# A trunk kernel: modulation rows computed four parts at a time, the first rows of h made in halves, and a pooling band matmul of 144 columns

## The chip, the cores and the metric

The kernel runs on one core of a Trainium2 chip. The metric is the device time of one execution in microseconds. The kernel before takes 1817.61 us (median of 3 runs, 1816.09 to 1818.15).

## The reference, cut to what matters

1024 tokens of 1024 features, two layers, all in float32. Each sub-layer normalizes, scales and shifts by rows made from one conditioning vector `c` (the modulation), and adds its gated result to x.

```python
c_act = jax.nn.silu(c)
for l in range(2):
    mod = c_act @ w_ada[l] + b_ada[l]          # (1, 6 * 1024), six parts
    sh_m, sc_m, g_m, sh_f, sc_f, g_f = jnp.split(mod, 6, axis=-1)
    h = rmsnorm(x, norm_mix_g[l]) * (1 + sc_m) + sh_m
    if l == 0:   # one projection to 2560 columns, gating in chunks of 128, a conv of width 3, w_out
        y = concat(chunk_sgu(u, v), short_gated_conv(b, c, x_in)) @ w_out_even[0]
    else:        # per group of 256 channels: mean over the last 2/4/8/16 tokens minus h, then a 256x256 map
        y = pool_mixer(h, w_pool[0], pool_scale[0])
    x = x + g_m * y
    h = rmsnorm(x, norm_ffn_g[l]) * (1 + sc_f) + sh_f
    x = x + g_f * hier_moe(h, ...)             # 32 experts, two per token
return rmsnorm(x, final_norm_g)
```

## The kernel before, in words

The program is written engine by engine, with semaphores between them; on each engine and each DMA queue the order is the order of the code. Large products are taken in a high part and a rest (names with `_hi`/`_lo`, "high" and "low" in the trace), three matmuls for one. There are six stages.

1. Start (to 42 us): x is loaded, squared and scaled on ScalarE, transposed on TensorE into `hT` ("h_columns"); VectorE sums the first two modulation parts.
2. Making h (to 67.5 us). For each of 8 blocks k of 128 features, [128 x 1024 tokens]: ScalarE writes the high part `h_hi`; VectorE writes the modulated `hT` in place (L1054) and, for even k, the rest `h_lo` (L1058); GpSimd writes `h_lo` for odd k (L645), as well as the rest of each weight piece (`piece_low`, L639). TensorE's first unit of the projection follows block by block.
3. Projection (to about 261 us). 16 pieces of weights w, two token halves each, so 32 units u of 24 matmuls of 512 columns (L1524 to L1526). ScalarE evicts units 0 to 23 (L837), loads the next piece and makes its high part. Beside it runs the modulation: ten parts, each of eight 512 KB loads on SP's queue (L486, `cond_w`, four buffers) and eight VectorE multiply-adds over [128 x 1024] (L1079). A part is then summed over the partitions by TensorE (`sum_part`, L1504, matmuls against ones), behind the unit that `PART_BEHIND` names (4, 6, 8, 10, 13, 15, 17, 19, 22, 24), and written out by ScalarE (`part_row`), some of them after VectorE has applied a gain (L1067). The load of the v weights on SP waits for the last sum.
4. v, the gating, the output projection, the residual and the rows for the experts, a tile of 128 tokens at a time.
5. The experts of layer 0 (to about 1055 us), then the pooling stage (1063 to 1152 us), then the experts of layer 1 and the last norm.
6. Of the pooling stage, iteration k works on several tiles. VectorE: `combine` of tile k (L1419, L1420), scaling of h for tile k-1 (L1433) and its shift (L1436, then `h_ready`), the entry rows for tile k-3 (L1150, L1152), the residual of tile k-2 (L1442). TensorE: band matmuls of tile k-1, for each of 8 blocks one of 128 columns (L1738) and one of 16 columns with the tile before (L1741), transposes and router logits of older tiles, then the group map of tile k-1 (L1754), which waits for `pool_kept` and for the residual of the tile before. ScalarE: squares, one eviction of the pooled columns (L996), eviction of transposes.

Of the kernel before, what the change touches and what calls it, by code (L numbers as in the profile page):

```python
# [45 lines left out]
def hybrid_trunk(nc, x, c, w_ada, b_ada, norm_mix_g, norm_ffn_g, w_in_even, sgu_norm_g, w_spatial,  # L46
# [6 lines left out]
    P = 128  # L53
# [48 lines left out]
    with ctx:  # L102
# [9 lines left out]
        C0 = T0 + 16 * KB + 256  # L112
# [6 lines left out]
        def small(name, shape, dt=F32):  # L119
            n = 4  # L120
            for s in shape[1:]:
# [19 lines left out]
        acc = [at(f"cond_acc{q}", [P, D], X0 + 4 * q * KB) for q in range(2)]  # L141
        bias = [at(f"cond_bias{q}", [P, D], X0 + (8 + 4 * q) * KB) for q in range(2)]
        CONDS = 4
        cond = [at(f"cond_w{q}", [P, D], X0 + (16 + 4 * q) * KB) for q in range(CONDS)]
        gain_in = at("gain_row_in", [1, D], T0 + 8 * KB)
        row_kept = at("mod_row", [1, D], T0 + 4 * KB)

        PARTS = [(0, m) for m in range(2, NMOD)] + [(1, m) for m in range(NMOD)]
        N0 = NMOD - 2
        GAIN_OF = {(0, SC_F): (norm_ffn_g[0:1, :], 1.0), (1, SC_M): (norm_mix_g[1:2, :], 1.0),  # L150
                   (1, G_M): (pool_scale[0:1, :], 0.0), (1, SC_F): (norm_ffn_g[1:2, :], 1.0)}
        GAINED = [n for n, q in enumerate(PARTS) if q in GAIN_OF]
        STORED = [n for n, q in enumerate(PARTS) if q not in ((0, G_M), (0, G_F))]

        PART_BEHIND = {4 + 9 * n // 4: n for n in range(len(PARTS))}


# [50 lines left out]
        band = at("band", [P, PG, P], T0 + 12 * KB)  # L208
        band0 = at("band_first", [P, PG, P], T0 + 14 * KB)
        band_prev = at("band_previous", [P, PG, REACH], T0 + 16 * KB)  # L210
# [73 lines left out]
        vec_rows = at("vector_rows", [P, P], T0)  # L284
        vec = small("vector_columns", [P, 64])
        c_e = small("c_exp", [P, KD])
        c_act = small("c_act", [P, KD])
# [34 lines left out]
        vc = vec[:, KD:2 * KD]  # L322
        NVEC = 2 * KD + 3 * KA

        def conv_col(k, m):
            return vec[:, 2 * KD + k * KA + m:2 * KD + k * KA + m + 1]
# [7 lines left out]
        PM = BANK[6]  # L334
        PL = BANK[7]
# [8 lines left out]
        bias_loaded = [sem(f"bias_loaded{q}") for q in range(2)]  # L344
# [7 lines left out]
        pool_loaded, rows1_loaded = sem("pool_loaded"), sem("rows1_loaded")  # L352
        rows0_loaded, ffn1_loaded = sem("rows0_loaded"), sem("ffn1_loaded")
# [19 lines left out]
        h_act, h_dve, h_pool = sem("h_act"), sem("h_dve"), sem("h_pool")  # L373
# [38 lines left out]
        h_ready, pool_T, pool_kept = sem("h_ready"), sem("pool_T"), sem("pool_kept")  # L412
# [7 lines left out]

        def h_made(k):

            return k + (k + 1) // 2 + 1
# [33 lines left out]
        def _(sp):  # L457
# [3 lines left out]
            sp.dma_start(vec_rows[2 * KD:NVEC, :],  # L461
# [16 lines left out]
            def part_loads(n):  # L478
                l, m = PARTS[n]
                if n >= 2:  # L480
                    sp.wait_ge(cond_used, KD * (n - 1))
# [16 lines left out]
            for n in range(len(PARTS)):  # L498
                part_loads(n)
            sp.wait_ge(part_summed, len(PARTS))  # L500
# [9 lines left out]
            for part, q0, n in zip(out_parts, (0, 4, 6, 7), (4, 2, 1, 1)):  # L510
                sp.dma_start(part[:, :, :], ow[:, q0:q0 + n, :]).then_inc(out_w_loaded, 16)
            sp.wait_ge(v_done, NT)
            sp.wait_ge(row_stored, 16 * len(STORED))
# [85 lines left out]
        def _(pool):  # L599
# [30 lines left out]
            g.sem_inc(consts, 1)  # L630
            pool.wait_ge(x_T, NT)
            for q in range(2):
                note(g.memset(bias[q][:, :], 0.0))
# [8 lines left out]
            piece_low(0)  # L642
            for k in range(1, KD, 2):
                pool.wait_ge(h_dve, h_made(k))
                g.tensor_tensor(h_lo[:, k, :], hT[:, k, :], h_hi[:, k, :].bitcast(F32), ALU.subtract).then_inc(h_pool, 1)  # L645
            for w in range(1, PIECES):
                piece_low(w)
# [24 lines left out]
            def bands():  # L672
# [17 lines left out]
                note(g.tensor_copy(band0[:, :, :], band[:, :, :]))  # L690
# [39 lines left out]
            for l in range(LAYERS):  # L730
                if l:
                    pool.wait_ge(h_ready, NT)
                    pool.wait_ge(x_mixed1, YB + 1)
                    clear_gathered()
# [35 lines left out]
        def _(act):  # L770
# [6 lines left out]

            act.wait_ge(vec_ready, 1)
            a.activation(c_e[:, :], vc, ACT.Exp, scale=-1.0).then_inc(c_exp_ready, 1)
# [21 lines left out]

            act.wait_ge(mod_ready0, 1)
# [6 lines left out]
            def load_gain(i):  # L809
                src = GAIN_OF[PARTS[GAINED[i]]][0]  # L810
                act.dma_start(gain_in[0:1, :], src).then_inc(gain_loaded, 16)
# [971 lines left out]
```

## Time and profile before

| | us |
|---|---|
| median of 3 runs | 1817.61 |
| profiled execution, its own time | 1813.75 |
| its span, first to last instruction | 1811.9 |
| TensorE busy | 1639.3 |
| VectorE busy | 1510.0 |
| ScalarE busy | 1030.9 |
| GpSimd busy | 437.1 |

The profile shows one execution. Busy shares are averages over stages with different limits, so what a change is worth is read from the stages that it touches. "Idle before <- X" tells how long an engine stood still and what released it. The clock column is the granted TensorE clock, 1.00 for 2.4 GHz and 0.50 for 1.2 GHz.

### The profile page before, as it was taken

To read this page: it belongs to the slowest core of one execution; us is meant where nothing else is said; L and a number is where in the kernel's file an instruction comes from. 1 tells how busy PE (TensorE), PEld (TensorE's weight loads), DVE (VectorE), ACT (ScalarE), POOL (GpSimd) and SP (SyncE) were. 2 spreads that over 40 slices of the span, in tenths; PEclk is the share of its full clock that TensorE was granted. 3 is DMA by queue.
4 is the path that set the end of the run, shared out by engine and by line. 5 is a ranking of instruction groups with operands and counts; after the bars stand their busy time and mean duration, and the time that the engine had idled before them with its cause. 6 is when DMAs were issued, how large, how long until landed. Compare 5 with 4: busy or idle time off the path is not lost. (4 is left out here: it accounts for less than half of the span.)

```text
span 1811.9 us, 20023 instructions
## 1 busy us (share of the span) xinstructions
PE 1639.3 (90%) x7847; PEld 1371.4 (76%) x7847; DVE 1510.0 (83%) x1095; ACT 1030.9 (57%) x840; POOL 437.1 (24%) x227
## 2 busy tenths in 40 slices
PE   3799999996899999999999949699999999999980
PEld 3577787785788888888888749678888888888870
DVE  5988785644699999999999758679999999999966
ACT  7221112322467777777777524357777777777742
POOL 1412130220424232322223100003432322233210
PEclk8799999997799999999999969789999999999995
DMA  9699712314699999999999954169999999999947
GB/s 340 203 314 314 266 69 81 119 46 197 218 343 376 381 385 390 385 383 387 381 388 388 387 210 173 49 234 365 381 388 387 387 383 384 384 384 387 386 183 285
DMA packets 125270, 547.62 MB, mean 302 GB/s; under 512 B 24003, under 2 KB 42975, under 8 KB 76021
## 3 DMA queue, kind: packets, MB, share of 16 engines
q1 hardware_dynamic: 91934, 497.98, 72.6%
q0 software_dynamic: 18432, 33.60, 4.9%
q10 hardware_dynamic: 14808, 14.73, 2.4%
q8 instruction: 64, 1.05, 0.2%
q14 instruction: 32, 0.26, 0.0%
HBM read 533.61 MB, written 46.17 MB: 320 GB/s over the span
## 5 line engine op out<-in xcount | busy, mean ns | idle before, releaser
L1310 DVE TENSOR_TENSOR unit_low<-unit,unit_high 128x2048 fp32r<-128x2048 f32 x384 | 856.0, 2283 | 15.3 <-ACT unit_high L924 15.0
L924 ACT ACTIVATE unit_high<-unit 128x2048 fp32r<-128x2048 f32 x384 | 735.4, 1915 | 42.6 <-DMA unit<-in_moe_w_up_dram 17.6
L1621 PE MATMUL ps<-unit_high,block_columns_high 128*128 128x512 f32 x1024 | 407.2, 398 | 10.4 <-DVE block_columns_low L1315 10.4
L714 POOL DMA_INDIRECT expert_rows<-y_out,assignment x64 | 214.8, 3357 | 804.3 <-DVE y_out L1340 791.9
L1623 PE MATMUL ps<-unit_high,block_columns_low 128*128 128x512 f32 x1024 | 401.2, 392 | 0.0
L1622 PE MATMUL ps<-unit_low,block_columns_high 128*128 128x512 f32 x1024 | 400.8, 391 | 0.0
L1621 PEld LDWEIGHTS ps<-unit_high,block_columns_high 128*128 128x128 f32 x1024 | 194.3, 190 | 50.2 <-DVE block_columns_low L1315 11.8
L1623 PEld LDWEIGHTS ps<-unit_high,block_columns_low 128*128 128x128 f32 x1024 | 193.5, 189 | 41.5
L1622 PEld LDWEIGHTS ps<-unit_low,block_columns_high 128*128 128x128 f32 x1024 | 193.8, 189 | 38.3
L1633 PE MATMUL ps<-unit_high,act_columns_high 128*128 128x512 f32 x512 | 206.7, 404 | 9.8 <-DVE unit_low L1310 9.8
L1635 PE MATMUL ps<-unit_high,act_columns_low 128*128 128x512 f32 x512 | 201.6, 394 | 0.0
L1634 PE MATMUL ps<-unit_low,act_columns_high 128*128 128x512 f32 x512 | 201.4, 393 | 0.0
L943 ACT ACTIVATE act_columns_high<-ps 128x512 fp32r<-128x512 f32 x64 | 38.4, 599 | 187.6 <-PE ps L1641 187.6
L708 POOL DMA_INDIRECT gathered<-normed_rows,token x64 | 110.7, 1730 | 140.5 <-issue 72.8
L1079 DVE SCALAR_TENSOR_TENSOR cond_acc<-cond_w,c_act,cond_acc 128x1024 f32<-128x1024 f32 x70 | 114.2, 1631 | 21.4 <-DMA cond_w<-in_w_ada_dram 14.2
L1315 DVE TENSOR_TENSOR block_columns_low<-ps,block_columns_high 128x1024 fp32r<-128x1024 f32 x64 | 78.2, 1222 | 53.5 <-ACT block_columns_high L873 53.3
L1524 PE MATMUL ps<-h_columns_high,in_w_high 128*128 128x512 f32 x256 | 107.8, 421 | 13.8 <-POOL h_columns_low L645 7.8
L1633 PEld LDWEIGHTS ps<-unit_high,act_columns_high 128*128 128x128 f32 x512 | 97.5, 190 | 28.6 <-issue 10.1
L1635 PEld LDWEIGHTS ps<-unit_high,act_columns_low 128*128 128x128 f32 x512 | 97.1, 190 | 20.9
L1634 PEld LDWEIGHTS ps<-unit_low,act_columns_high 128*128 128x128 f32 x512 | 97.4, 190 | 18.7
L1526 PE MATMUL ps<-h_columns_high,in_w_low 128*128 128x512 f32 x256 | 102.2, 399 | 0.0
L1525 PE MATMUL ps<-h_columns_low,in_w_high 128*128 128x512 f32 x256 | 102.1, 399 | 0.0
(225 smaller groups left out, 1962.6 us busy)
## 6 DMA issues: line engine op xcount, KB each, us to landing
unit<-in_moe_w_gate_dram SPq DMA_DIRECT2D x128, 1024.0 KB, 7.7
unit<-in_moe_w_up_dram SPq DMA_DIRECT2D x128, 1024.0 KB, 7.3
unit<-in_moe_w_down_dram SPq DMA_DIRECT2D x128, 1024.0 KB, 8.5
cond_w<-in_w_ada_dram SPq DMA_DIRECT2D x80, 512.0 KB, 5.2
y_in<-expert_rows SPq DMA_DIRECT2D x16, 1024.0 KB, 7.3
x_rows<-in_x_dram SPq DMA_DIRECT2D x8, 1024.0 KB, 9.9
cond_w<-in_w_ada_dram SPq DMA_DIRECT2D x8, 1024.0 KB, 11.1
in_w<-in_w_in_even_dram ACTq DMA_DIRECT2D x12, 512.0 KB, 7.9
```

The costliest lines, as they stand in the source:

```text
L708: g.indirect_dma_start(out=dst[:, :], out_offset=None, in_=xn_dram[l], in_offset=bass.IndirectOffsetOnAxis(ap=index, axis=0), bounds_check ...
L714: g.indirect_dma_start(out=y_dram[l], out_offset=bass.IndirectOffsetOnAxis(ap=index, axis=0), in_=src[:, :], in_offset=None, bounds_check= ...
L924: a.activation(high[k][:, :], raw[i % SLOTS][:, :], ACT.Copy).then_inc(unit_high, 1)
L1079: ch.link(v.scalar_tensor_tensor(out=acc[n % 2][:, :], in0=cond[k % CONDS][:, :], scalar=c_act[:, k:k + 1], in1=acc[n % 2][:, :] if k else ...
L1310: v.tensor_tensor(low[i % SLOTS][:, :], raw[i % SLOTS][:, :], high[k][:, :].bitcast(F32), ALU.subtract)\
L1524: mm(BANK[u % 4], w_hi, h_hi[:, k, tokens], start=k == 0, stop=False)
L1621: mm(dst, xT_hi[:, q, :], high[k][:, cols], start=q == 0, stop=False)
L1622: mm(dst, xT_hi[:, q, :], low[i % SLOTS][:, cols], start=False, stop=False)
L1623: last = mm(dst, xT_lo[:, q, :], high[k][:, cols], start=False, stop=q == KD - 1)
L1633: mm(BANK[2 + half], aT_hi[:, q, :], high[k][:, cols], start=q == 0, stop=False)
L1634: mm(BANK[2 + half], aT_hi[:, q, :], low[i % SLOTS][:, cols], start=False, stop=False)
L1635: last = mm(BANK[2 + half], aT_lo[:, q, :], high[k][:, cols], start=False, stop=q == KF - 1)
```

## The change

- Modulation: the ten parts become three groups (`QUADS`) of four, four and two parts. In a buffer of [128 x 1024] each part has 32 (or 64) partitions of its own, filled by one DMA per part. The vector c is laid out to match (six more small loads on ScalarE's queue at the start). A group is summed by matmuls against a [128 x 4] or [128 x 2] matrix behind units 13, 21 and 24, its rows are finished by one VectorE operation and stored by one DMA from SP. There are five buffers in place of four. The gain rows of layer 0 are read back from DRAM.
- Making h: by token halves. ScalarE also modulates `hT` for odd k, VectorE makes all of `h_lo` and the rest of pieces 0 and 1. The first units run in the order (piece 0, half 0), (1, 0), (0, 1), (1, 1).
- Pooling: one matmul of 144 columns per block; its last 16 columns are the next tile's share, which ScalarE keeps in `carry` and VectorE adds to the next tile's pooled columns (`pool_whole`). The shift of h is on GpSimd.
- In layer 0 the router logits of tile k-2 stand ahead of the transposes of tile k-1.

The core of the diff:

```diff
-                sp.dma_start(bias[n % 2][0:1, :], b_ada[l:l + 1, m * D:(m + 1) * D]).then_inc(bias_loaded[n % 2], 16)
-                for k in range(KD):
-                    if KD * n + k >= CONDS:
-                        sp.wait_ge(cond_used, KD * n + k - CONDS + 1)
-                    sp.dma_start(cond[k % CONDS][:, :],
-                                 w_ada[l].rearrange("(k p) n -> k p n", p=P)[k, :, m * D:(m + 1) * D])\
-                      .then_inc(cond_loaded[k % CONDS], 16)
+                for g in range(D // rows):
+                    if i >= CONDS:
+                        sp.wait_ge(cond_used, i - CONDS + 1)
+                    for j in range(parts):
+                        sp.dma_start(cond[i % CONDS][j * rows:(j + 1) * rows, :],
+                                     w_ada[l, g * rows:(g + 1) * rows, (m0 + j) * D:(m0 + j + 1) * D])\
+                          .then_inc(cond_loaded[i % CONDS], 16)
+                    i += 1
...
+            for n, (l, m0, parts) in enumerate(QUADS):
+                sp.wait_ge(row_out, n + 1)
+                sp.dma_start(mod_dram[l][m0:m0 + parts, :], mod_rows[n][0:parts, :]).then_inc(row_stored, 16)
+            sp.wait_ge(part_summed, len(QUADS))
...
+                    for t in range(NT):
+                        pool.wait_ge(h_scaled, t + 1)
+                        g.tensor_tensor(h_r[t % 2][:, :], h_r[t % 2][:, :], b1b[:, :], ALU.add).then_inc(h_ready, 1)
...
-                    a.activation(pooledT[:, :, :], PA[0].rearrange("p (k q) -> p k q", q=P), ACT.Copy)\
-                     .then_inc(pool_kept, 1)
+                    for q0, n in ((0, 6), (6, 2)):
+                        dst = pooledT[:, q0:q0 + n, :]
+                        last = a.activation(dst.rearrange("p (b q) c -> p b q c", q=3) if n == 6 else dst,
+                                            span_of(q0, n, slice(0, P)), ACT.Copy)
+                    last.then_inc(pool_kept, 1)
+                    for q0, n in ((0, 6), (6, 2)):
+                        dst = carry[(k - 1) % 2][:, q0:q0 + n, :]
+                        last = a.activation(dst.rearrange("p (b q) c -> p b q c", q=3) if n == 6 else dst,
+                                            span_of(q0, n, slice(P, SPAN)), ACT.Copy)
+                    last.then_inc(carry_kept, 1)
...
+            for half in range(2):
+                tokens = slice(half * CH, (half + 1) * CH)
+                for b in range(KD // 2):
+                    k = 2 * b
+                    dve.wait_ge(h_act, 12 * half + 3 * b + 1)
+                    v.tensor_scalar(hT[:, k, tokens], hT[:, k, tokens], a_m[:, k:k + 1], mod_c[:, SH_M, k:k + 1],
+                                    ALU.mult, ALU.add).then_inc(h_dve, 1)
+                    if b:
+                        dve.wait_ge(h_act, 12 * half + 3 * b)
+                        h_rest(k - 1, half)
+                    dve.wait_ge(h_dve, 4 * half + b + 1)
+                    h_rest(k, half)
...
-                    ch.link(v.scalar_tensor_tensor(out=h_r[t % 2][:, :], in0=xr[:, t, :],
-                                                   scalar=rstd[:, N_MIX1, t:t + 1], in1=a1b[:, :],
-                                                   op0=ALU.mult, op1=ALU.mult))
-                    v.tensor_tensor(h_r[t % 2][:, :], h_r[t % 2][:, :], b1b[:, :], ALU.add).then_inc(h_ready, 1)
+                    v.scalar_tensor_tensor(out=h_r[t % 2][:, :], in0=xr[:, t, :],
+                                           scalar=rstd[:, N_MIX1, t:t + 1], in1=a1b[:, :],
+                                           op0=ALU.mult, op1=ALU.mult).then_inc(h_scaled, 1)
+                if 2 <= k < NT + 1:
+                    t = k - 1
+                    dve.wait_ge(pool_kept, t + 1)
+                    dve.wait_ge(carry_kept, t)
+                    v.tensor_tensor(pooledT[:, :, 0:REACH], pooledT[:, :, 0:REACH], carry[1 - t % 2][:, :, :], ALU.add)\
+                     .then_inc(pool_whole, 1)
                 if 0 <= k - 3:
                     entry_rows(1, k - 3)
...
                     for q in range(KD):
-                        g = q // 2
-                        part = PA[0][:, q * P:(q + 1) * P]
-                        last = mm(part, h_r[t % 2][:, q * P:(q + 1) * P], (band if t else band0)[:, g, :],
-                                  start=True, stop=t == 0)
-                        if t:
-                            last = mm(part[:, 0:REACH], h_r[1 - t % 2][:, q * P:(q + 1) * P], band_prev[:, g, :],
-                                      start=False, stop=True)
+                        last = mm(span_cols(q), h_r[t % 2][:, q * P:(q + 1) * P],
+                                  (band_all if t else band0_all)[:, q // 2, :], start=True, stop=True)
```

## Rows read from the trace of the kernel before

**Rows 1.** Timeline of the pooling stage, VectorE (start us, duration us, instruction).
```profile
1102.14 1.28 DVE L1433 SCALAR_TENSOR_TENSOR h_rows<-x_rows,rstd,scale_row 128x1024 f32<-128x1024 f32 x1
1103.46 1.23 DVE L1436 TENSOR_TENSOR h_rows<-h_rows,shift_row 128x1024 f32<-128x1024 f32 x1
1105.28 0.17 DVE L1147 RECIPROCAL rstd<-root_mean_square 128x1 f32<-128x1 f32 x1 [0.60 <-ACT root_mean_square L776]
...
1111.66 1.28 DVE L1433 SCALAR_TENSOR_TENSOR h_rows<-x_rows,rstd,scale_row 128x1024 f32<-128x1024 f32 x1
...
1145.48 1.22 DVE L1442 TENSOR_TENSOR x_rows<-x_rows,ps 128x1024 f32<-128x1024 f32 x1
```

**Rows 2.** Timeline of the pooling stage, TensorE.
```profile
1071.49 3.75 PE L1738 MATMUL ps<-band_first,h_rows 128*128 128x128 f32 x16 [19.64 <-DVE h_rows L1436]
...
1106.53 0.38 PE L1738 MATMUL ps<-band,h_rows 128*128 128x128 f32 x2
1106.75 0.29 PE L1741 MATMUL ps<-band_previous,h_rows 128*128 128x16 f32 x2
...
1112.68 3.70 PE L1754 MATMUL ps<-pool_w,pooled_columns 128*128 128x256 f32 x16
1116.22 0.38 PE L1738 MATMUL ps<-band,h_rows 128*128 128x128 f32 x2
```

**Rows 3.** Timeline of the projection, VectorE.
```profile
62.42 1.27 DVE L1079 SCALAR_TENSOR_TENSOR cond_acc<-cond_w,c_act,cond_bias 128x1024 f32<-128x1024 f32 x1
...
76.96 2.81 DVE L1079 SCALAR_TENSOR_TENSOR cond_acc<-cond_w,c_act,cond_acc 128x1024 f32<-128x1024 f32 x1 [0.52 <-DMA cond_w<-in_w_ada_dram]
...
218.39 1.21 DVE L1067 SCALAR_TENSOR_TENSOR mod_row<-ps,gain_row_in 1x1024 f32<-1x1024 f32 x1 [0.36 <-DVE cond_acc L1079]
```

**Rows 4.** Busy times by window: us, PE, PEld, DVE, ACT, POOL, clock, DMA, GB/s.
```profile
47.70:67.50 19.80, 11.95 (x25) 7.42 (x26) 19.40 (x13) 5.63 (x6) 13.47 (x5) 0.50 0.39 134
...
100.00:130.00 30.00, 30.00 (x123) 22.77 (x122) 24.54 (x17) 6.07 (x9) 5.90 (x3) 1.00 0.92 318
```

**Rows 5.** Timeline from making h on, all engines.
```profile
43.23 9.15 ACT L805 ACTIVATE h_columns_high<-h_columns,mod_columns,a_mix 128x1024 fp32r<-128x1024 f32 x8
...
46.34 1.23 DVE L1058 TENSOR_TENSOR h_columns_low<-h_columns,h_columns_high 128x1024 fp32r<-128x1024 f32 x1
...
49.05 3.26 DVE L1058 TENSOR_TENSOR h_columns_low<-h_columns,h_columns_high 128x1024 fp32r<-128x1024 f32 x1
...
61.70 0.80 DVE L1054 TENSOR_SCALAR h_columns<-h_columns,a_mix,mod_columns 128x1024 f32<-128x1024 f32 x1
...
65.95 0.80 PE L1524 MATMUL ps<-h_columns_high,in_w_high 128*128 128x512 f32 x1 [2.27 <-POOL h_columns_low L645]
```

**Rows 6.** Timeline of the projection, ScalarE: evictions of units 2 and 3.
```profile
79.27 0.60 ACT L837 ACTIVATE conv_in<-ps 128x512 f32<-128x512 f32 x1 [3.54 <-PE ps L1526]
84.71 0.60 ACT L837 ACTIVATE conv_in<-ps 128x512 f32<-128x512 f32 x1 [4.84 <-PE ps L1526]
```

**Rows 7.** Timeline of TensorE: the sums behind units 19 and 24.
```profile
187.49 2.85 PE L1504 MATMUL ps<-cond_acc,ones 128*128 128x512 f32 x4 [2.61 <-DVEq L1084]
...
219.95 1.88 PE L1504 MATMUL ps<-cond_acc,ones 128*128 128x512 f32 x4
```

**Rows 8.** DMA issue of line 486 (ns), a window of 1 us, page's GB/s.
```profile
L486 SPq DMA_DIRECT2D cond_w<-in_w_ada_dram x80: 327/328/595, 47.8 to 212.3; - x80
...
229.00:230.00 1.00, 1.00 (x6) 0.85 (x5) 1.00 (x1) 0.00 (x0) 1.00 (x1) 1.00 1.01 345
...
GB/s 340 203 314 314 266 69 81 119 46 197 218 343 376 381 385 390 385 383 387 381 388 388 387 210 173 49 234 365 381 388 387 387 383 384 384 384 387 386 183 285
```

**Rows 9.** Timelines of GpSimd and ScalarE: an unhindered GpSimd subtraction, the pooled eviction.
```profile
176.08 2.39 POOL L639 TENSOR_TENSOR in_w_low<-in_w,in_w_high 128x1024 fp32r<-128x1024 f32 x1 [12.45 <-ACT in_w_high L799]
...
1083.59 1.02 ACT L996 ACTIVATE pooled_columns<-ps 128x1024 f32<-128x1024 f32 x1 [5.93 <-PE ps L1741]
```

**Rows 10.** A window of 2 us in the pooling stage, columns as in group 4.
```profile
1094.00:1096.00 2.00, 2.00 (x6) 1.65 (x5) 1.97 (x3) 1.62 (x4) 0.00 (x0) 0.50 0.96 330
```

More of the change, by code:

```diff
@@ L630, in _ @@
             g.sem_inc(consts, 1)
+            for i, tile in enumerate((pick4, pick2)):
+                note(g.memset(tile[:, :], 0.0))
+            for tile in mod_rows:
+                note(g.memset(tile[:, :], 1.0))
+            settle()
+            for parts in (4, 2):
+                for j in range(parts):
+                    rows = P // parts
+                    note(g.memset(pick[parts][j * rows:(j + 1) * rows, j:j + 1], 1.0))
+                settle()
             pool.wait_ge(x_T, NT)
-            for q in range(2):
-                note(g.memset(bias[q][:, :], 0.0))
+            for tile in acc:
+                note(g.memset(tile[:, :], 0.0))
             settle()
@@ L640, in piece_low @@
                                 piece_hi[w % HRING][:, :, :].bitcast(F32), ALU.subtract).then_inc(w_low, 1)
[L642 to L646, printed above, removed]
+            for w in range(2, PIECES):
                 piece_low(w)
@@ new lines, in _ @@
+            for half in range(2):
+                tokens = slice(half * CH, (half + 1) * CH)
+                for b in range(KD // 2):
+                    k = 2 * b
[7 more added lines that the diff above has]
+                    h_rest(k, half)
+                    if half == 0 and b == 1:
+                        piece_low(1)
+                dve.wait_ge(h_act, 12 * half + 12)
+                h_rest(KD - 1, half)
@@ new lines, in quad_sum @@
+            def quad_sum(n, i):
+                l, m0, parts = QUADS[n]
+                dve.wait_ge(bias_loaded, 16 * sum(q[2] for q in QUADS[:n + 1]))
+                for g in range(D * parts // P):
+                    dve.wait_ge(cond_loaded[i % CONDS], 16 * sum(PARTS_OF[i % CONDS:i + 1:CONDS]))
+                    ch.link(v.scalar_tensor_tensor(out=acc[n][:, :], in0=cond[i % CONDS][:, :],
+                                                   scalar=c_of[parts][:, g:g + 1], in1=acc[n][:, :],
@@ L1093, in conv @@
+            i = 0
+            for n in range(len(QUADS)):
+                i = quad_sum(n, i)
+                if n:
+                    quad_rows(n - 1)
+            quad_rows(len(QUADS) - 1)
             def conv(m):
@@ new lines, in project @@
+                if u >= 4:
+                    done = u - 3
+                    pe.wait_ge(*((proj_kept, done) if done <= 6 * KA else (z_kept, done - 6 * KA)))
+                tokens = slice(half * CH, (half + 1) * CH)
+                for k in range(KD):
+                    if u in (0, 2):
+                        pe.wait_ge(h_low, half * KD + k + 1)
+                    w_hi, w_lo = piece_hi[w % HRING][:, k, :], piece_lo[w % RING][:, k, :]
+                    mm(BANK[u % 4], w_hi, h_hi[:, k, tokens], start=k == 0, stop=False)
+                    mm(BANK[u % 4], w_hi, h_lo[:, k, tokens], start=False, stop=False)
+                    last = mm(BANK[u % 4], w_lo, h_hi[:, k, tokens], start=False, stop=k == KD - 1)
@@ L1531, in _ @@
+                last.then_inc(proj_done, 1)
+                if u in QUAD_BEHIND:
+                    sum_quad(QUAD_BEHIND[u])
             pe.wait_ge(x_T_kept, NT)
             pe.wait_ge(mod_ready0, 1)
-            for w in range(PIECES):
-                project(w)
+            for u in range(2 * PIECES):
+                project(u)
             pe.wait_ge(ws_loaded, 16)
-            pe.wait_ge(row_out, len(PARTS))
+            pe.wait_ge(row_out, len(QUADS))
             for h in range(HEADS):
@@ L1582, in _ @@
             pe.wait_ge(conv_done, 1)
-            for k in range(NT + 2):
+            for k in range(NT + 1):
                 if k < NT:
```

264 lines of the change are left out of this document (120 added, 144 removed).

## The prediction, made before the change was run

> **What bounds the kernel now.** I read the busy times by window first, then the timeline of each stage that the change touches, engine by engine, and asked who is late last in each. Three stages matter.
>
> In the making of h TensorE runs at 1.2 GHz (clock 0.50) and is busy 11.95 of 19.80 us, VectorE 19.40 [rows 4]. TensorE's last gap there ends with GpSimd's rest at 65.95 [rows 5]. VectorE's own rests take 1.23 us where GpSimd is quiet and share 3.26 us with it otherwise (the second is at 49.05) [rows 5]: the two engines hinder each other, so GpSimd's help costs VectorE almost as much as it takes over.
>
> In the projection two streams run side by side and end together. TensorE needs 5.44 us for a unit (84.71 - 79.27) [rows 6]. The modulation stream on VectorE starts at 62.42 and ends at 218.03, where the last gained row waits 0.36 us before 218.39 [rows 3]: 155.6 us for 80 multiply-adds, 1.945 us each. One alone takes 1.27 us, one beside GpSimd 2.81 us, and VectorE also waits for loads [rows 3]; in a window of this stage the DMA engines are 0.92 busy at 318 GB/s and VectorE is busy 24.54 of 30 us [rows 4]. TensorE already waited 2.61 us for that stream before the sum at 187.49 [rows 7], and starts the last sum at 219.95, which ends at 221.8 [rows 7].
>
> In the pooling stage TensorE is the bound, barely. From one tile's band matmuls to the next it takes 9.69 us (1116.22 - 1106.53) [rows 2]. VectorE's period, from scaling to scaling, is 9.52 us with 0.60 us of waiting in it [rows 1], so 8.9 us of work. The reader is to see here that VectorE runs ahead of the band matmuls: it hands h over and goes on to older tiles.
>
> **The change, part by part.**
>
> *Start.* Six small loads on ScalarE's queue and a larger transpose. What is late next there are the x loads and the first weights; I take 0, with 0 to 1.5 us as bounds (six issues of 0.33 us at most are 2 us, the price of an issue in [rows 8]).
>
> *Making h in halves.* A half of a block is 512 columns: for VectorE about 0.7 us for a rest (1.23 for 1024) and 0.45 for a modulation (0.80 for 1024) [rows 5]. A half of h is 8 x 0.7 + 4 x 0.45 = 7.4 us, with 1.2 us for the rest of piece 1 and 0.6 us of handoffs 9.2 us for the first half and 8 us for the second. ScalarE has 12 passes of 0.60 us [rows 6] and one of about 1.0 us per first half, 8.2 us: just ahead. ScalarE began at 43.23 in the old kernel [rows 5], behind the high part of piece 0, which is now made earlier; so VectorE starts near 42.5, the first half is there at 51.7, the second at 59.9. GpSimd is quiet, so nothing is hindered. TensorE ends unit 0 near 53, unit 1 near 60.3 (its first matmuls at the low clock), unit 3 near 71.3. It was at 84.7 [rows 6]: 13 us ahead.
>
> *Modulation.* Still 80 multiply-adds over [128 x 1024] and the same bytes. Gone are seven of ten sums on TensorE: 7 x 1.88 = 13 us [rows 7], ScalarE's row passes, and all but one row operation inside VectorE's stream. Without waits TensorE would end unit 24 at 71.3 + 21 x 5.44 + 2 x 1.88 = 189.3. But the stream decides. Its first multiply-add is at 60; three row operations of about 1.5 us with handoff come off the 155.6 us, which leaves (155.6 - 4.5) / 80 = 1.89 us each. So group 0 is done at 120.5 (unit 13 ends at 125.7, in time), group 1 at 181 (unit 21 ends at 171: TensorE waits 10 us), group 2, with one row operation, at 60 + 151.1 + 1.5 = 212.6; the fifth buffer should take a little off, I say 211. The last sum ends at 213.2, and the restart after a gap costs 1 to 2 us (2.85 against 1.88 for a sum of the same size [rows 7], and more behind it); I take 1.7. Gain at this point: 221.8 - 213.2 - 1.7 = 7 us. All that follows (units 25 to 31, convolution, v) is shifted whole. The v load now stands on SP behind three waits for finished rows and three stores, some 2 us later after the last sum; it had time for that, since ScalarE takes it up four units on.
>
> SP's queue issues four DMAs for one: 4 x 0.328 = 1.31 us [rows 8] per group of 512 KB, below the pace of 1.89, so I cost it at nothing; if the pace fell below 1.4 us it would be next. What a transfer onto 32 partitions costs, the trace doesn't show. Bounds: nothing, and twice the time (the second rival). The nearest row is the window 229 to 230, in which the eight loads of the spatial bias, onto 64 partitions each, are at work with others: 345 GB/s at a DMA share of 1.01 [rows 8], no sign of a loss. I take nothing.
>
> *Pooling stage, TensorE.* The 128-column matmul pair takes 0.22 us (1106.75 - 1106.53) [rows 2], 144 columns 0.25 us; 8 blocks take 2.0 us where the old pairs of pairs took 3.5. TensorE's period would fall from 9.7 to 8.2 us. That is worth nothing, because of the next step.
>
> *Pooling stage, VectorE.* The shift (1.23 us [rows 1]) leaves for GpSimd, a small add of 128 columns comes (0.3 us; a 1024-column pass is 1.23 us). But the add is put directly behind the scaling of h, and it waits for the pooled columns of the very tile that was just scaled. In the old order nothing on VectorE waited for that tile before the next iteration but one. Now, in each of the seven iterations k = 2 to 8, VectorE stands still while: GpSimd shifts (2.39 us for a pass of that size, unhindered since VectorE idles [rows 9]), TensorE runs 8 blocks (2.0 us), ScalarE evicts in two passes (1.02 for 1024 columns [rows 9], 0.60 for 512 [rows 6], so 0.80 + 0.39, 1.1 us overlapped), the add itself (0.3) and four handoffs of 0.1. Sum 6.2 us. Queued behind that wait are the entry rows of tile k-3, the residual of tile k-2 and the next combine; the group map on TensorE waits for that residual. VectorE's other work is 8.9 - 1.2 = 7.7 us. New period 13.9 us against 9.7: 4.2 us more, seven times 29, less 2.4 us because the last such iteration has no combine: 27 us. That is with TensorE at 2.4 GHz. At 1.2 GHz the band takes 3.75 us for 128 columns [rows 2], 4.2 for 144: 2.2 us more per tile, 15 in all, and 3.6 us on the last group map (3.70 at full clock [rows 2]), 46 us in sum. The old stage already had a stretch at 0.50 with TensorE hardly ever idle [rows 10]; now gaps near 3 us come twice in each period. I take half of the band's loss: 35 us. Nothing hides it: the next experts start from the last tile's residual, which ended at 1146.7 [rows 1].
>
> *Router logits ahead of the transposes*: the last ones no longer queue behind one another, -0.5 us.
>
> **Sum.** 1813.75 (profiled execution) + 35 - 7 - 0.5 = 1841.2 us. The median of the runs, 1817.6, lies 3.9 us above the profiled execution, so 1845 us, 1.5% slower.
>
> **Rivals.**
> 1. *The stream runs free (faster side).* Place: the sums behind units 21 and 24. If the five buffers let the stream go at 1.61 us or less per multiply-add ((189.3 - 60) / 80), TensorE never waits and the last sum ends at 191.2, 30.6 us early. With the pooling stage at its cheap end, 27 us, that gives 1817.6 - 30.6 + 27 - 0.5 = 1813.5. For it: the DMA engines move 390 GB/s with expert weights [rows 8], 1.35 us for 512 KB. Against it: 14 passes of GpSimd that each take 1.5 us from VectorE (2.81 - 1.27 [rows 3]) add 14 x 1.54 / 80 = 0.27 to 1.27, and each handoff to the next pass about 0.15: 1.69. Between the forecast and this lies a time within 0.2% of before.
> 2. *The quarter transfers collide.* If a transfer onto 32 partitions gets half of the 385 GB/s of the expert stages [rows 8], a group takes 524 KB / 192 GB/s = 2.73 us, the stream ends at 278, 67 us later than forecast: 1912 us. Against it stands the window at 345 GB/s; for it, that no row has two engines writing to so few partitions with rows of 4 KB. The Trainium skill, SBUF — State Buffer, section Door 1, speaks against the change here: a transfer onto partitions 0 to 31 reaches 8 of 16 ports and was measured at 189 GB/s against 328 for 128 partitions, and two transfers to different halves serialize; by its figure a group would take 2.77 us, an estimate, and the end would be near 1915. No run here shows it yet.
> 3. *The pooling stage stays at the low clock*: 46 for 35 us, 1856. Inside the range.
> 4. *The change does not do what it says*: making h is no faster because ScalarE or the handoffs lag. The stream then starts at 62.4 and ends 2.4 us later: 1847. The 13 us at unit 3 are swallowed by the stream anyway.
>
> **How the numbers follow.** Chances: forecast with its bounds (pooling 27 to 46, stream end 201 to 228, which is 1.75 to 2.1 us per multiply-add) 0.77, with rivals 3 and 4 in it, from 1845 - 8 - 10 = 1827 to 1845 + 11 + 17 = 1873; rival 2, whole or in part, 0.14; rival 1 or near it 0.09. Range 1824 to 1880. Below 1814.0 (faster by over 0.2%, about what a measurement can tell) 0.06, within 0.2% 0.03, slower by over 0.2% 0.91.
>
> **What would show it.** In the new pooling stage: VectorE idle about 5.5 to 8 us before the small add, released by ScalarE, seven times; a period of 14 to 16 us; GpSimd passes of 2.4 us. In the projection: unit 3's eviction near 72; TensorE idle before the second and third sum; the last sum near 211. Wrong would be the forecast if VectorE's idle time ahead of the add were under 2 us, if the multiply-adds came at 1.6 us or at 2.4 us or more.

## The result, and the profile after

| us | before | after |
|---|---|---|
| median of 4 runs each | 1817.88 | 1876.15 (1865.06 to 1879.43) |
| profiled execution, its own time | 1813.75 | 1875.03 |
| its span | 1811.9 | 1873.1 |
| VectorE busy | 1510.0 | 1490.9 |
| first reduce of the v stage | 268.26 | 299.53 |
| pooling stage, first combine to last entry rows | 88.2 | 118.8 |

The kernel got slower: ratio 1.0311, interval 1.0267 to 1.0354. The sign was forecast and the time lies in the range, but the loss is 58 us where 27 were predicted. The last two rows of the table say where it is: 31.3 us before the v stage and 30.6 us in the pooling stage, together 61.9 us, against 61.3 us between the two profiled executions. The second had been predicted (35); of the first, the opposite (7 us of gain).

The projection. First the timelines (start us, duration us, instruction), ScalarE's evictions of units 2 and 3, then VectorE and TensorE:

```profile
68.15 0.60 ACT L857 ACTIVATE conv_in<-ps 128x512 f32<-128x512 f32 x1 [4.03 <-PE ps L1569]
73.60 0.60 ACT L857 ACTIVATE conv_in<-ps 128x512 f32<-128x512 f32 x1 [3.85 <-PE ps L1569]
...
63.90 11.77 DVE L1112 SCALAR_TENSOR_TENSOR cond_acc<-cond_w,c_act,cond_acc 128x1024 f32<-128x1024 f32 x7
...
240.38 1.28 DVE L1112 SCALAR_TENSOR_TENSOR cond_acc<-cond_w,c_act,cond_acc 128x1024 f32<-128x1024 f32 x1 [1.31 <-DMA cond_w<-in_w_ada_dram]
...
249.23 1.27 DVE L1125 SCALAR_TENSOR_TENSOR mod_rows_of<-ps,ident,mod_rows_of 4x1024 f32<-4x1024 f32 x1 [0.32 <-DVE cond_acc L1112]
...
141.43 3.58 PE L1551 MATMUL ps<-cond_acc,pick_quarter 128*4 128x512 f32 x4 [13.42 <-DVEq L1117]
```

The waits between 60 and 255 us (us in total, times, longest), the windows (columns as in [rows 4]) and SP's issues of the stream (ns, min/median/max) with their landings:

```profile
DVE cond_acc L1112 <- DMA cond_w<-in_w_ada_dram: 64.6, 58, 2.8
...
PE ps L1551 <- DVEq L1117: 52.6, 3, 25.9
...
100.00:130.00 30.00, 28.01 (x124) 22.87 (x122) 17.46 (x13) 5.61 (x8) 5.04 (x2) 1.00 1.06 242
130.00:160.00 30.00, 18.57 (x65) 12.78 (x66) 15.15 (x13) 3.20 (x4) 4.42 (x2) 0.72 1.06 247
...
L499 SPq DMA_DIRECT2D cond_w<-in_w_ada_dram x48: 310/421/1611, 100.6 to 129.5; - x48
...
DMA to landing us min/median/max: 7.4/9.1/10.7
```

TensorE is 11 us ahead at unit 3, against [rows 6]. Then the stream takes over: 13 multiply-adds of 1.3 us fit into the window from 100 to 130, and between them VectorE waits for loads. The DMA engines are busier (a share of 1.06, all of the time, against 0.92) and bring less (242 against 318 GB/s) [rows 4]. The 80 multiply-adds last until 248.9 against 218.0 [rows 3], TensorE stands still for them three times, 52.6 us in all, and in the next window its clock falls to 0.72.

The pooling stage, one period of VectorE and what lies in it:

```profile
1122.03 1.28 DVE L1476 SCALAR_TENSOR_TENSOR h_rows<-x_rows,rstd,scale_row 128x1024 f32<-128x1024 f32 x1
1123.39 2.34 POOL L764 TENSOR_TENSOR h_rows<-h_rows,shift_row 128x1024 f32<-128x1024 f32 x1 [14.73 <-DVE h_rows L1476]
1125.79 2.23 PE L1780 MATMUL ps<-band,h_rows 128*128 128x144 f32 x16 [0.74 <-POOL h_rows L764]
1128.05 1.08 ACT L1015 ACTIVATE pooled_columns<-ps 128x768 f32<-128x768 f32 x2 [4.62 <-PE ps L1780]
1129.02 0.35 ACT L1020 ACTIVATE carried_columns<-ps 128x96 f32<-128x96 f32 x2
1129.17 0.29 DVE L1483 TENSOR_TENSOR pooled_columns<-pooled_columns,carried_columns 128x128 f32<-128x128 f32 x1 [5.86 <-ACT pooled_columns L1015]
...
1135.75 1.29 DVE L1476 SCALAR_TENSOR_TENSOR h_rows<-x_rows,rstd,scale_row 128x1024 f32<-128x1024 f32 x1
```

The chain GpSimd, TensorE, ScalarE runs while VectorE waits 5.86 us for its small add. The period is 13.72 us against 9.52 [rows 1]. The first of these waits is longer (11.86 us, shown below).

### The profile page after: what moved, and what is told of

It is laid out like the page before. It is cut to its first block and busy times, and to the rows that moved or that the text cites. A ratio compares the mean times of both kernels' runs of the same rounds, so it can differ in the third digit from the quotient of the medians.

```text
span 1873.1 us, 20010 instructions
## 1 busy us (share of the span) xinstructions
PE 1632.9 (87%) x7707; PEld 1360.3 (73%) x7707; DVE 1490.9 (80%) x1107; ACT 1037.1 (55%) x874; POOL 430.3 (23%) x241
## 5 line engine op out<-in xcount | busy, mean ns | idle before, releaser
L743 POOL DMA_INDIRECT expert_rows<-y_out,assignment x64 | 197.4, 3084 | 819.4 <-DVE y_out L1383 819.4
L737 POOL DMA_INDIRECT gathered<-normed_rows,token x64 | 114.7, 1792 | 138.0 <-issue 70.2
L1567 PE MATMUL ps<-h_columns_high,in_w_high 128*128 128x512 f32 x256 | 102.7, 401 | 4.0 <-DVE h_columns_low L1086 4.0
```

Of the source, the lines that this page charges most:

```text
L737: g.indirect_dma_start(out=dst[:, :], out_offset=None, in_=xn_dram[l], in_offset=bass.IndirectOffsetOnAxis(ap=index, axis=0), bounds_check ...
L743: g.indirect_dma_start(out=y_dram[l], out_offset=bass.IndirectOffsetOnAxis(ap=index, axis=0), in_=src[:, :], in_offset=None, bounds_check= ...
L1567: mm(BANK[u % 4], w_hi, h_hi[:, k, tokens], start=k == 0, stop=False)
```

## The experiments

Each was run beside the kernel before on the same chip; its medians there lay between 1816.4 and 1818.3 us.

**1. The pooling part alone.** The kernel before with the 144-column band, the carried columns, the early add and the shift on GpSimd, nothing else of the change.

> The kernel before with the pooling part of the change alone (144-column band matmuls, carried edge, small add on VectorE right behind the scaling of h, shift on GpSimd). Theory: VectorE stands still for the just-scaled tile in seven iterations, so this part alone costs what the stage grew by in the changed kernel: 30 us, 1848 us, with a period of 13.7 us in the stage. Rival: the stage only grew because the projection before it shifted something (DMA, clock); then this kernel costs under 15 us.

Measured: 1845.03 us, 28.4 more than before (ratio 1.0161, 1.0144 to 1.0178), with the same 5.86 us ahead of the add:

```profile
1103.53 1.28 DVE L1457 SCALAR_TENSOR_TENSOR h_rows<-x_rows,rstd,scale_row 128x1024 f32<-128x1024 f32 x1
1110.68 0.29 DVE L1464 TENSOR_TENSOR pooled_columns<-pooled_columns,carried_columns 128x128 f32<-128x128 f32 x1 [5.86 <-ACT pooled_columns L1014]
```

So this half of the loss arises without the other, and it is the one that was predicted.

**2 and 3. The split alone, as blocks and interleaved.** The kernel before, each 512 KB load in four DMAs; `sl` is `slice(32 * j, 32 * (j + 1))` in the first kernel and `slice(j, P, 4)` in the second, for partitions and source rows alike (the count that VectorE waits for follows, here and in the later splits).

```diff
-                    sp.dma_start(cond[k % CONDS][:, :], ...[k, :, m * D:(m + 1) * D])
+                    for j in range(4):
+                        sp.dma_start(cond[k % CONDS][sl, :], ...[k, sl, m * D:(m + 1) * D])
```

> The kernel before with one thing changed: each 512 KB modulation load is split into four DMAs, onto partitions 0-31, 32-63, 64-95 and 96-127; the same rows, the same places, the same arithmetic. If the split alone slows the stream to the 2.3 to 2.55 us per multiply-add of the changed kernel, the last sum ends 25 to 45 us later and the kernel takes 1843 to 1863 us. Rival: the loss comes from the new layout in DRAM order (each quarter reads 32 rows of another part) or from the five buffers; then this kernel stays within 5 us of before.

> As the split into four DMAs, same count and size (128 KB, 32 rows of 4 KB), but each DMA writes every fourth partition (0, 4, 8, ... and so on), so that it reaches over all 128. Theory A (the span of a transfer's partitions sets its rate): back to the pace of before, 1.95 us per multiply-add, 1818 us within 5 us. Theory B (four issues and completions for one cost the time): as slow as the split into blocks, 1843 us or more.

Measured: 1857.14 us (+40.5) as blocks, 1867.19 (+50.5) interleaved. The split by itself costs what the change lost, but interleaving did not heal it. The traces show that the two are slow for different reasons. Window from 100 to 130, issues and landing, blocks:

```profile
100.00:130.00 30.00, 22.52 (x81) 15.86 (x80) 17.42 (x12) 4.08 (x6) 5.09 (x2) 0.83 1.07 241
...
L487 SPq DMA_DIRECT2D cond_w<-in_w_ada_dram x46: 310/421/1366, 99.9 to 129.1; - x46
...
DMA to landing us min/median/max: 3.3/5.7/8.3
```

and interleaved:

```profile
100.00:130.00 30.00, 24.62 (x93) 17.84 (x91) 16.59 (x12) 3.78 (x5) 5.28 (x2) 0.89 0.76 233
...
L487 SPq DMA_DIRECT2D cond_w<-in_w_ada_dram x46: 469/594/1517, 99.7 to 129.7; - x46
...
DMA to landing us min/median/max: 2.3/2.7/4.7
```

With blocks the DMA engines are full (1.07) at 241 GB/s. Interleaved they have room (0.76), each transfer lands in 2.7 us, and SP hands out one every 0.65 us (30 / 46): 2.6 us for the four of a group. SP waits for a free buffer during only 1.5 us of this window, with blocks during 10.0 us. So SP's issues set the pace in the interleaved kernel, and the transfers in the other. So far that rests on one trace of each.

**4. The small add behind the residual**, in the changed kernel.

```diff
-                if 2 <= k < NT + 1:      # small add, directly behind the scaling of h
...
                     v.tensor_tensor(xr[:, t, :], xr[:, t, :], PA[1], ALU.add).then_inc(x_mixed1, 1)
+                if 2 <= k < NT + 1:      # the same lines, last in the iteration
```

> The changed kernel with the small add of the carried columns moved on VectorE from behind the scaling of h to the end of the iteration, behind the residual. Theory: the stall of 5.9 us per tile shrinks to about nothing; what stays is GpSimd's shift, 2.4 us beside VectorE's passes, of which VectorE loses about 1.5 us per tile. Period 10 us in place of 13.7, so 25 us less: 1850 us. Rival: VectorE then waits as long at the end of the iteration because TensorE's group map starts later; then under 8 us less.

Measured: the profiled execution took 1850.73 us, 24 less than that of the changed kernel; the four others took 1861 to 1867, median of the five 1865.8. By the medians the move is worth only 10 us here, where 25 had been expected. VectorE's idle time ahead of the add is gone in the trace, the period is 9.93 us, and two other rows catch the eye:

```profile
1130.38 1.28 DVE L1476 SCALAR_TENSOR_TENSOR h_rows<-x_rows,rstd,scale_row 128x1024 f32<-128x1024 f32 x1
1131.75 2.34 POOL L764 TENSOR_TENSOR h_rows<-h_rows,shift_row 128x1024 f32<-128x1024 f32 x1 [7.60 <-DVE h_rows L1476]
1131.77 3.39 DVE L1193 SCALAR_TENSOR_TENSOR modulate_tmp<-x_rows,rstd,ffn_scale_row 128x1024 f32<-128x1024 f32 x1
...
1137.52 0.29 DVE L1489 TENSOR_TENSOR pooled_columns<-pooled_columns,carried_columns 128x128 f32<-128x128 f32 x1
```

While GpSimd shifts, VectorE's next pass takes 3.39 us in place of 1.28, a loss of 2.1 us where the expectation had 1.5. What held up the four other executions, no trace shows. In runs 10 and 8 the same move was worth 27.5 and 21.6 us by the medians.

**5 and 6. Halves in place of quarters**, to take SP's issues out of the question: two DMAs of 256 KB per load, as blocks (partitions 0 to 63, 64 to 127) and interleaved (even, odd).

> The kernel before, each 512 KB modulation load split into two DMAs, onto partitions 0-63 and 64-127. In the run with four neighbouring quarters the DMA engines were 1.02 to 1.07 busy at 241 GB/s; in the run with four interleaved quarters only 0.68 to 0.78 busy at about the same rate, with SP's issues at a median of 594 ns each. Theory A2 (two limits: packets onto a few neighbouring partitions are slow, and separately SP's issues cost 0.3 to 0.6 us each): the halves show the first limit alone, weaker: DMA share near 1.0, stream pace near 2.08 us as in the last group of the changed kernel, time 1825 to 1835. Theory B (only the number of DMAs costs): two per group are cheap, time 1817 to 1822, with a DMA share as in the kernel before (0.92).

> The kernel before, each 512 KB modulation load split into two DMAs, one onto the even and one onto the odd partitions. Theory A2: the packets are as fast as in the kernel before, and two issues of 0.6 us are below the pace of 1.9 us, so 1815 to 1821, faster than the two neighbouring halves by 8 us or more. Theory B (only the number of DMAs costs): the same time as the two neighbouring halves. If interleaved rows are themselves slow (each source row apart), it is slower than the neighbouring halves.

Measured: 1860.95 us as blocks (ratio 1.0230, 1.0201 to 1.0259), 1817.03 interleaved (1.0002, 0.9991 to 1.0013). The same count of DMAs, the same bytes, 44 us apart. Blocks, then interleaved:

```profile
100.00:130.00 30.00, 18.96 (x70) 13.31 (x70) 17.48 (x12) 3.78 (x5) 4.38 (x2) 0.85 1.02 239
```

```profile
100.00:130.00 30.00, 30.00 (x124) 22.87 (x122) 24.77 (x17) 5.23 (x7) 5.00 (x2) 1.00 0.93 319
```

The interleaved row equals that of the kernel before (0.92, 318) [rows 4]. The expectation of the size was wrong, though: I had thought the blocks of 64 milder than those of 32, and they cost as much.

**12. A block in the middle.** Three DMAs, onto partitions 0 to 31, 32 to 95 and 96 to 127.

> The kernel before, each 512 KB modulation load split into three DMAs, onto partitions 0-31, 32-95 and 96-127. Split at 64 (0-63, 64-127) the time was 1861 us with the DMA engines 1.02 busy at 239 GB/s; split into even and odd partitions it was 1817 at 0.93 and 319 GB/s. Theory N (neighbouring partitions are slow as such): the middle block of 64 is as slow as the others, so 1857 to 1862 at about 240 GB/s, as with four quarters. Theory P (partitions 64 apart lie behind different ports, partitions 32 apart behind the same, as the Trainium skill's table has it): the middle block reaches all of them, half the bytes go at full speed and half at the slow one, so 1825 to 1845 at 265 to 300 GB/s. Theory B (only the count of DMAs): three should lie between two (1817, interleaved) and four (1867, interleaved): 1820 to 1860 whatever the blocks, which these rows alone don't tell from P but for the DMA share, near 0.8 by B and near 1.0 by P.

Measured: 1853.01 us (1843.77 to 1857.38; ratio 1.0178, 1.0140 to 1.0217), between what theories N and P had expected. The profiled execution, 1857.38, was as slow as with quarters:

```profile
100.00:130.00 30.00, 24.91 (x93) 18.14 (x92) 18.82 (x13) 4.12 (x6) 6.47 (x2) 0.89 1.03 245
130.00:160.00 30.00, 27.03 (x108) 20.30 (x106) 17.51 (x14) 5.15 (x7) 5.53 (x2) 0.94 1.06 229
```

By the port table of the Trainium skill (SBUF — State Buffer, section Door 1) the middle block reaches every port, as the even or the odd partitions do. For the middle block these rows do not bear it out: 265 GB/s or more had been expected of it. A small effect can't be excluded, since two executions took 1844 and 1850 us and the stream of the profiled one ended at 257.1 us against 260.2 with quarters; and the middle block always ran beside two blocks of 32, never alone.

**13 and 14. Destination and source taken apart.** Two DMAs again. In the first the partitions are blocks and the source rows interleaved, in the second the reverse; c is laid out to match.

```diff
+  (13)  sp.dma_start(cond[k % CONDS][slice(64 * j, 64 * (j + 1)), :], ...[k, slice(j, P, 2), ...])
+  (14)  sp.dma_start(cond[k % CONDS][slice(j, P, 2), :], ...[k, slice(64 * j, 64 * (j + 1)), ...])
```

> The kernel before, each 512 KB modulation load split into two DMAs, with destination and source taken apart: the destinations are partitions 0-63 and 64-127, the sources the even and the odd rows of the weights (c is laid out to match, which adds up to 1 us at the start). Where both were blocks the time was 1861 us at 239 GB/s, where both were interleaved 1817 at 319 GB/s, and a middle block (32-95) did not help in the profile (245 and 229 GB/s). Theory D (it is the destination: neighbouring partitions): as the blocks, 1854 to 1866 at about 240 GB/s. Theory S (it is the source: rows that are read together lie too near to each other in HBM): as the interleaved one, 1815 to 1823 at about 315 GB/s.

> The counterpart: the destinations are the even and the odd partitions, the sources rows 0-63 and 64-127 of each block of weights. Theory D (destination): fast, 1815 to 1823 at about 315 GB/s. Theory S (source): slow, 1854 to 1866 at about 240 GB/s. If both this and its counterpart lie between, both sides have a part in it.

Measured: 1860.76 us (1.0231, 1.0192 to 1.0270) with blocks as destination, 1816.33 (0.9997, 0.9984 to 1.0009) with interleaved partitions. The windows, in this order:

```profile
100.00:130.00 30.00, 19.84 (x71) 13.68 (x70) 18.03 (x12) 3.78 (x5) 4.79 (x2) 0.84 1.04 236
```

```profile
100.00:130.00 30.00, 30.00 (x125) 22.93 (x123) 24.48 (x17) 5.84 (x8) 5.71 (x3) 1.00 0.91 316
```

It is the destination alone. Whether the source rows of a transfer are neighbours or alternate makes no difference.

**7 and 8. One DMA for a group, parts outermost.** The changed kernel (8: with the late add as well) with one DMA in place of four.

```diff
+                    sp.dma_start(cond[i % CONDS][:, :],
+                                 w_ada[l, g * rows:(g + 1) * rows, m0 * D:(m0 + parts) * D]
+                                 .rearrange("r (j n) -> j r n", j=parts))
```

> The changed kernel with the four (or two) loads of a group made one DMA of 512 KB: the same rows on the same partitions, all 128 at once. Theory A2: stream pace back to 1.9 us (1.85 to 2.0), last sum near 213 instead of 251, time 1876 - 36 = 1840 (1836 to 1850), with the start 1.9 us later and the pooling stage 30 us longer still in it. If the layout of four parts itself, or rows of 4 KB at four places of the source, were slow, it stays at 1865 to 1880. If the size of the gain is decided elsewhere (TensorE's clock after the waits), 1850 to 1865.

> The changed kernel with one DMA per group and the small add of the carried columns behind the residual of the tile before. The pooling period was 9.93 us with the add there against 13.72 in the changed kernel, so both mendings together give 1840 - 26 = 1814 (1806 to 1826). Below 1813 it beats the kernel before. Rival: the later stages give part of it back, as the four unprofiled runs of the kernel with the late add alone do (1861 to 1867 against 1851 for its profiled execution): 1825 to 1835.

Measured: 2186.32 and 2164.70 us. All 128 partitions are filled at once, and it is far slower; 1840 and 1814 us had been expected. The share of the stream's queue, in a window of the first group (four parts) and of the last (two parts), and the issues:

```profile
q1 hardware_dynamic: 656, 2.61, 22.4%
...
q1 hardware_dynamic: 391, 1.58, 12.8%
...
L498 SPq DMA_DIRECT2D cond_w<-in_w_ada_dram x80: 522/5350/11407, 50.8 to 526.5; - x80
```

With the parts outermost the queue keeps 22.4% of 16 engines busy, about four of them, and with two parts 12.8%, about two (that only the stream's DMAs are confined is read from this share; which engines they use is not in the trace). The Trainium skill has this as a rule (DMA: Bandwidth & Descriptors, Rules for kernel authors): an outermost dimension smaller than 16 confines a DMA to at most that many engines. These rows agree.

**9 and 10. One DMA for a group, rows outermost.** Row r of part j goes to partition 4r + j (2r + j for two parts); c and the summing matrix are laid out to match. Run 10 has the late add too; it came out 1.5 us below its expected range.

```diff
+                                 .rearrange("r (j n) -> r j n", j=parts))
```

> The changed kernel with one DMA of 512 KB per group whose source runs row by row (row r of part j goes to partition 4r + j, so the outermost count is 32 or 64 and each row's four pieces lie on neighbouring partitions); c and the summing matrix are laid out to match (two small copies and two small sums more on VectorE at the start). With the parts outermost (count 4) one such DMA took 5.38 us of issue and the DMA engines were 0.24 busy. Theory (a DMA is dealt out to the engines by its outermost count, and a short count or a few neighbouring partitions leave most of the machinery unused): with 32 or 64 outermost the stream runs at 1.85 to 2.0 us per multiply-add at a DMA share near 0.92, the last sum ends near 213, and the time is 1876 - 36 = 1840 us (1834 to 1850), the pooling stage unmended. Rival: a source with two dimensions is slow by itself; then issues stay above 3 us each and the time above 1900.

> As the run before, with the small add of the carried columns behind the residual of the tile before. Its period in the pooling stage was 9.93 us in the kernel with that move alone, against 13.72. So 26 us less than the run before: 1814 (1808 to 1826), level with the kernel before. If the projection gives part of it back, above 1826.

Measured: 1834.01 us (1.0099, 1.0080 to 1.0118) and 1806.53 (0.9944, 0.9926 to 0.9961). From run 9:

```profile
100.00:130.00 30.00, 30.00 (x130) 23.35 (x128) 27.18 (x19) 6.44 (x9) 5.22 (x4) 1.00 0.97 345
...
L501 SPq DMA_DIRECT2D cond_w<-in_w_ada_dram x18: 534/535/546, 101.4 to 129.9; - x18
...
205.75 1.27 DVE L1128 SCALAR_TENSOR_TENSOR mod_rows_of<-ps,ident,mod_rows_of 4x1024 f32<-4x1024 f32 x1 [0.32 <-DVE cond_acc L1115]
```

The stream ends at 205.4 instead of 248.9, at 345 GB/s; the first reduce of the v stage comes at 255.43, 44.1 us earlier than in the changed kernel and 12.8 earlier than before. That is so although the start is 3.0 us later than before (the copy of the first modulation columns stands at 44.74 against 41.75). With this one repair the first half of the loss is not only gone but turned into the gain that the change is able to give.

**11. The shift back on VectorE**, on top of run 10.

> As the run before, with the shift of the rows back on VectorE. With the shift on GpSimd (2.34 us) VectorE's next scaling took 3.39 us in place of 1.28 and VectorE was busy 29.6 of 30 us. So a period gets 1.2 us longer by the shift and 2.1 us shorter by the undisturbed scaling: 9.0 us in place of 9.93, seven times, 6 us less than the run before: 1808 (1800 to 1818), faster than the kernel before. Rival: TensorE or the group map becomes the bound at once, or the two are equal: no change within 2 us.

Measured: 1801.49 us, 0.9910 of the kernel before (0.9893 to 0.9928), the fastest version. Its rows in the pooling stage:

```profile
1085.02 1.28 DVE L1475 SCALAR_TENSOR_TENSOR h_rows<-x_rows,rstd,scale_row 128x1024 f32<-128x1024 f32 x1
1086.34 1.23 DVE L1478 TENSOR_TENSOR h_rows<-h_rows,shift_row 128x1024 f32<-128x1024 f32 x1
...
1087.67 1.28 DVE L1192 SCALAR_TENSOR_TENSOR modulate_tmp<-x_rows,rstd,ffn_scale_row 128x1024 f32<-128x1024 f32 x1
...
1094.05 1.28 DVE L1475 SCALAR_TENSOR_TENSOR h_rows<-x_rows,rstd,scale_row 128x1024 f32<-128x1024 f32 x1
```

The pass of 3.39 us is back at 1.28, the period is 9.03 us, and the stage takes 84.4 us against 88.2 before. The gain over run 10 is 5.0 us (6 expected).

## Why the prediction came out as it did, step by step

*Start.* Taken at 0, bounds 0 to 1.5. Measured 1.9: a copy of the first modulation columns stands at 43.68 against 41.75. The six issues on ScalarE's queue take 2.75 us and the transpose waits for their landing until 8.94. The bound counted the issues, not the landing.

*Making h.* Right. Unit 3 was forecast to end near 71.3 and its eviction began at 73.60, of which 1.9 us are the start. It brought nothing by itself, as the prediction said: the stream decides.

*Modulation stream.* This is the step that failed. It was to end at 211 and ended at 248.9, and the point where the v stage begins moved by +31.3 us in place of -7. The failed sentence is the one on what a transfer onto 32 partitions costs: "I take nothing". Runs 2 and 5 put the price at 40 and 44 us in the kernel before, and run 9 gives 42 us back in the changed one (1876.15 - 1834.01). The row behind that sentence, 345 GB/s in the window from 229 to 230 [rows 8], is one microsecond in which those loads run among others, and nothing in it tells which transfers moved the bytes. They are eight loads of 32 KB, and the v load of 2048 KB was under way beside them. The microsecond behind it looks quite different:

```profile
230.00:231.00 1.00, 1.00 (x6) 0.81 (x5) 1.00 (x1) 0.00 (x0) 0.88 (x1) 1.00 0.77 190
```

A share of 1.01 should have made me suspicious: full DMA engines at 345 GB/s, where the expert stages reach 390 [rows 8], is no free resource.

*Rival 2* was the cause, with too small a chance (0.14) and too high a price: 2.73 us a group and a stream until 278. Measured are 2.3 us in the mean over 80 ((248.9 - 63.90) / 80). Its rate was close in the window from 100 to 130. It took 192 GB/s for the stream, and the stream's queue moved 6.09 MB in these 30 us, 203 GB/s (queue, packets, MB, share of the 16 engines):

```profile
q1 hardware_dynamic: 2230, 6.09, 87.7%
```

But the rate did not stay so low (all queues together moved 270 and 283 GB/s from 160 to 190 and from 190 to 220, against the 242 here), so the mean price is lower. As to the mechanism, the Trainium skill (SBUF — State Buffer, section Door 1) says that 64 partitions get no more than 32, and runs 2 and 5 agree (241 and 239 GB/s). The same page of the Trainium skill (section "Can I just issue two DMAs to hit both halves?") says that only one transfer over all 128 partitions reaches every port. Runs 6 and 14 disagree with that, two interleaved halves move 319 and 316 GB/s. The measurements decide: what counts here is whether the partitions of a transfer are spread over all 128, not how many there are.

*SP's four issues* were taken at 0.328 us and nothing. They measured 0.42 us, 1.7 us for four, still below the pace. That they were not the bound in the changed kernel is seen from SP's own waits for a free buffer between 60 and 255 us (us in total, times, longest), from the full DMA engines (1.06) and from run 5, which loses as much with half as many issues:

```profile
SPq L499 <- DVEq L1115: 51.7, 49, 6.1
```

Run 3 shows that they are next as soon as the packets run freely, there with 0.59 us each. In the prediction they had a threshold (1.4 us a group); the price of an issue that it used was that of the full load.

*Without the transfer's price* the modulation term had the right sign but was too small: forecast 7 us of gain, measured 12.8 in run 9, and that with a start 3.0 us late, so near 16. There the multiply-adds come at 1.74 us ((205.4 - 64.95 - 1.6) / 80, with 1.6 for the row operation inside and its handoff) in place of 1.89, since VectorE waits for hardly any load.

*Pooling stage.* Right: 30.6 us measured, 35 forecast (27 with TensorE at full clock), and run 1 gives 28.4 for it alone. The terms: shift 2.34 (2.39), band 2.23 (2.0), eviction of the columns 1.08 (1.1), idle time 5.86, period 13.72 (13.9). The 8 us for a low clock were mostly too much. The band matmuls of tiles 1 to 7 took 286 ns each in the median, those of the first tile 447, so on VectorE's path only the first iteration paid. Its group map took 5.72 us, with the clock at 0.50 until 1112 us (3.70 at full clock [rows 2]), and behind it VectorE's first wait was twice as long as the others:

```profile
1109.26 5.72 PE L1795 MATMUL ps<-pool_w,pooled_columns 128*128 128x256 f32 x16 [1.17 <-ACT pooled_columns L1015]
...
1118.10 0.29 DVE L1483 TENSOR_TENSOR pooled_columns<-pooled_columns,carried_columns 128x128 f32<-128x128 f32 x1 [11.86 <-ACT pooled_columns L1015]
```

Rival 3 did not happen. The shift on GpSimd was costed at what it takes there; that it also makes VectorE's next pass 2.1 us longer was hidden by the wait and shows as soon as that is gone (runs 4 and 11).

*Median against profile.* 1.1 us, where 3.9 were added.

In sum: +1.9 (start) and +29.4 (stream) where 0 and -7 stood, and +30.6 where 35 stood. The stream and the start are off by 38 us, the pooling term and the median by 4 and 3 the other way, and the gain of 0.5 us from the router logits was not measured by itself. That the time still lies in the range is luck: the error of that step alone is larger than the whole width above the forecast (35 us), and two smaller errors took 7 us of it back.

## What to carry to other kernels

Splitting one load into several onto blocks of neighbouring partitions can cost a quarter of the DMA rate at the same bytes; if parts must come from different places, interleave them over the partitions, and let the outermost dimension of the one DMA that brings them be large (32 and 64 were fast here, 4 and 2 slow). A small operation that waits for the newest tile belongs at the end of the iteration, behind all that does not depend on it. And a window of one microsecond with mixed traffic is no evidence that a resource is free: take the row of a stage in which the thing in question is alone or dominant, or keep its price open in the range.

## What the runs showed of the hardware that I had not expected

- Two DMAs onto even and odd partitions go as fast as one over all (319 against 318 GB/s), two onto 0-63 and 64-127 at 239. Source order makes no difference (runs 13 and 14: 236 and 316). The middle block, 32 to 95, gave no clear relief between two blocks of 32; it was not run alone. Why neighbouring partitions are slow is left open: how a transfer's rows are dealt to the DMA engines is not in these traces.
- A DMA with an outermost dimension of 4 keeps its queue at 22.4% of the engines, one with 2 at 12.8%, and SP's issue of it takes 5.35 us (median) in place of 0.54.
- An interleaved quarter costs SP 0.594 us to issue, a quarter as a block 0.421, the full load 0.328.
- A GpSimd pass of 2.34 us stretches the VectorE multiply beside it from 1.28 to 3.39 us: it takes nearly its whole length from it.
